# A quarter of the second expert table moved from TensorE to gathered rows and running sums on VectorE

## The chip, the core and the metric

The kernel runs on one core of one Trainium2 chip. A core has TensorE (PE in the profile, with PEld for its weight loads), VectorE (DVE), ScalarE (ACT), GpSimd (POOL) and SyncE (SP), each with its own instruction stream, and 16 DMA engines that all queues share. The engines meet only at semaphores. The metric is the device time of one execution in microseconds, as the median of several runs.

## The reference

One block of a streaming encoder on 256 tokens of width 2048 in float32. A token-mixing part (pooling and differential attention) is followed by the part that matters here, a retrieval of single-neuron experts. There are 16384 experts (128 x 128); each token picks 16 of them in each of 8 heads, so 128 per token:

```python
s1 = jnp.einsum('bshc,kc->bshk', q[..., 0, :], keys1)
s2 = jnp.einsum('bshc,kc->bshk', q[..., 1, :], keys2)
v1, i1 = lax.top_k(s1, PEER_TOPK)
v2, i2 = lax.top_k(s2, PEER_TOPK)
cand = v1[..., :, None] + v2[..., None, :]
vals, pos = lax.top_k(cand, PEER_TOPK)          # ids = i1 * 128 + i2 of the winners
gates = jax.nn.softmax(vals, axis=-1)
ug = jnp.take(u_tab, ib, axis=0)
vg = jnp.take(v_tab, ib, axis=0)
h = jnp.einsum('td,tkd->tk', xb, ug)
a = jax.nn.gelu(h, approximate=False) * gb
f = jnp.einsum('tk,tkd->td', a, vg)
```

The block then adds f and a gated embedding to the residual and normalizes each token's row of 2048 values.

## The kernel before

Nothing is gathered. The kernel computes the hidden value of every expert for every token, multiplies it by a gate that is zero for experts not picked, and multiplies the result by the whole second table.

**Units.** All weights stream through the core in units of 128 x 1024 float32 (512 KB): SP loads a unit into one of four slots of RAW, ACT rounds it to HI (L436), DVE subtracts to get the remainder LO (L713), and PE multiplies HI by the high and the low part of the activations and LO by the high part (t_unit, L1181, L1182, L1186, with the weights stationary in PE; n_unit, L1199 and L1206, with the activations stationary and the table moving). SP may load slot u % 4 when LO of unit u - 4 is made. ACT works three units ahead of PE and DVE one; LO has two slots.

**First half of U.** 64 blocks of 128 experts (two units each). ACT writes the GELU of each block to BUF (L650), which has 128 blocks of 128 experts x 256 tokens. DVE meanwhile finds the 16 winners of each head (tk0 to tk7).

**Gate stage: second half of U.** For each block of U, PE also multiplies pairs of one-hot matrices (L1435), which gives for four tokens the gates of all 128 x 128 experts. DVE makes the one-hots (L1072, L1074), multiplies GELU into BUF (L1085, from PSUM) and multiplies the gates into BUF for four tokens (L1089). After it BUF holds GELU times gate for everything. Blocks of BUF that no GELU has written yet are first filled with ones by POOL (L410, L412).

**Table stage.** 128 blocks, two units each. For block k, ACT copies BUF block k to XH (L684), DVE makes XL (L1125), each with two slots, and PE multiplies by 128 rows of the second table (in_peer_v). In the order of ACT and of DVE the split of a block stands ahead of that block's conversions, which belong to later units (vt_body). The sums stay in PSUM for the whole stage. POOL brings back the residual and the last layer norm's weights in 16 pieces (L421, L423), and at the end DVE adds the residual (L1145) and normalizes.

The order of all work is written out by hand, per engine; loops (Fori) repeat it.

## Time and profile before

| | |
|---|---|
| median of 3 runs | 2465.26 us (2464.59 to 2473.16) |
| the profiled execution | span 2465.7 us |
| PE busy | 2328.1 us (94%) |
| DVE busy | 1546.4 us (63%) |
| ACT busy | 1028.8 us (42%) |
| POOL busy | 72.6 us (3%) |
| mean DMA traffic | 172 GB/s |
| first half of U | about 868 to 1255 us |
| gate stage | about 1255 to 1688 us |
| table stage | 1692 to 2444 us |

Busy shares are means over stages with different limits; a stage is read in its own window. The end of a matmul in the profile is modelled, so the pace of PE is read from the starts of matmuls in a row. The clock that TensorE was granted is given as a share of full speed.

### The profile page before, as it was taken

How to read it: one execution, taken by the hardware profiler on the slowest of the kernel's cores; microseconds unless marked ns; L12 is line 12 of the kernel's file. 1: busy time of each engine (PE TensorE's matmuls, PEld its weight loads, DVE VectorE, ACT ScalarE, POOL GpSimd, SP SyncE). 2: the span in 40 equal slices, each digit the busy share in tenths (PEclk: the TensorE clock that was granted, in tenths of full speed). 3: DMA queues.
4: the chain of work that ended last, by engine and by line, in shares of the span. 5: the costliest groups of instructions: out<-in, count | busy, mean ns of one | idle time of the engine just before them, and what ended most of it. 6: DMA issues, size and time to landing. Idle time of an engine off the chain costs nothing.

```text
span 2465.7 us, 46080 instructions
## 1 busy us (share of the span) xinstructions
PE 2328.1 (94%) x15504; PEld 2129.6 (86%) x15504; DVE 1546.4 (63%) x2726; ACT 1028.8 (42%) x1390; POOL 72.6 (3%) x64
## 2 busy tenths in 40 slices
PE   4999999999899979999999999999999999999996
PEld 4999999898698879999999999998777777777775
DVE  4446555665744587777789889886444444444446
ACT  2444555544444434444433333333444444434442
POOL 0000000000100040000000000000000000000000
PEclk9999999999999989999999999999999999999998
DMA  6654555455455645555544554555556666665553
GB/s 176 191 183 157 183 173 173 155 179 186 152 174 162 187 158 181 181 183 182 183 140 156 159 160 154 159 160 161 180 180 184 185 188 187 189 179 187 184 187 119
DMA packets 116574, 425.25 MB, mean 172 GB/s; under 512 B 13840, under 2 KB 13856, under 8 KB 115520
## 3 DMA queue, kind: packets, MB, share of 16 engines
q1 hardware_dynamic: 112608, 412.14, 52.6%
q0 software_dynamic: 3936, 12.71, 2.1%
q8 instruction: 19, 0.31, 0.0%
q14 instruction: 11, 0.09, 0.0%
HBM read 418.50 MB, written 6.29 MB: 172 GB/s over the span
## 4 chain that ended last, share of the span: by engine, by line
PE 74%; DMA 12%; DVE 8%; issue 4%; ACT 2%; DVEq 0%; ACTq 0%; SPq 0%
PE ps L1186 17%; PE ps L1181 17%; PE ps L1182 16%; PE ps L1199 14%; DMA raw<-in_peer_v 10%; PE ps L1206 7%; DVE w_lo L713 3%; PE ps L1435 2%; DMA raw<-in_w_in 1%; DVE x_t_lo L1125 1%; ACT x_t_hi L684 1%; DMA ln_gb<-in_ln_in 1%; DVE bn L726 0%; PE ps L1307 0%; DVE tk_ab L1015 0%
## 5 line engine op out<-in xcount | busy, mean ns | idle before, releaser
L713 DVE TENSOR_TENSOR w_lo<-raw,w_hi 128x1024 fp32r<-128x1024 f32 x774 | 958.7, 1240 | 642.6 <-PE ps L1206 352.1
L436 ACT ACTIVATE w_hi<-raw 128x1024 fp32r<-128x1024 f32 x774 | 820.5, 1061 | 1118.0 <-DMA raw<-in_peer_v 371.0
L1181 PE MATMUL ps<-x_t_hi,w_hi 128*128 128x256 f32 x3328 | 836.5, 289 | 18.7 <-ACT v_t L486 12.2
L1182 PE MATMUL ps<-x_t_lo,w_hi 128*128 128x256 f32 x3328 | 821.3, 284 | 0.0
L1181 PEld LDWEIGHTS ps<-x_t_hi,w_hi 128*128 128x128 f32 x3328 | 642.2, 193 | 23.6 <-ACT w_hi L436 14.4
L1182 PEld LDWEIGHTS ps<-x_t_lo,w_hi 128*128 128x128 f32 x3328 | 642.9, 193 | 0.0
L1186 PE MATMUL ps<-x_t_hi,w_lo 128*128 128x256 f32 x3328 | 470.9, 284 | 15.3 <-DVE w_lo L713 15.3
L1186 PEld LDWEIGHTS ps<-x_t_hi,w_lo 128*128 128x128 f32 x3328 | 432.1, 193 | 16.8 <-DVE w_lo L713 16.7
L1199 PE MATMUL ps<-w_hi,x_t_hi 128*128 128x512 f32 x1024 | 324.6, 398 | 35.0 <-DVE x_t_lo L1125 34.3
L1199 PE MATMUL ps<-w_hi,x_t_lo 128*128 128x512 f32 x1024 | 317.6, 391 | 0.0
L1206 PE MATMUL ps<-w_lo,x_t_hi 128*128 128x512 f32 x1024 | 275.1, 391 | 0.0
L1199 PEld LDWEIGHTS ps<-w_hi,x_t_hi 128*128 128x128 f32 x1024 | 186.6, 188 | 100.0 <-issue 55.1
L1199 PEld LDWEIGHTS ps<-w_hi,x_t_lo 128*128 128x128 f32 x1024 | 192.9, 188 | 41.3
L1206 PEld LDWEIGHTS ps<-w_lo,x_t_hi 128*128 128x128 f32 x1024 | 193.3, 189 | 40.8
L1125 DVE TENSOR_TENSOR x_t_lo<-experts,x_t_hi 128x256 fp32r<-128x256 f32 x128 | 54.5, 426 | 114.5 <-ACT x_t_hi L684 114.5
L1089 DVE TENSOR_TENSOR experts<-ps,experts 128x512 f32 (+1 forms) x64 | 87.6, 1369 | 13.2 <-DVE experts L1085 13.1
L1199 PE MATMUL ps<-w_hi,a_hi 128*128 128x512 f32 x272 | 87.5, 403 | 8.3 <-DVE a_lo L925 4.0
L1074 DVE TENSOR_SCALAR onehots<-iota,i_t,gate_t 128x128 f32<-128x128 bf16 x256 | 92.7, 362 | 0.0
L1072 DVE TENSOR_SCALAR onehots<-iota,i_t 128x128 f32<-128x128 bf16 x256 | 77.5, 303 | 17.7 <-DVE experts L1089 13.2
L1199 PE MATMUL ps<-w_hi,a_lo 128*128 128x512 f32 x272 | 87.0, 401 | 0.0
L1435 PE MATMUL ps<-onehots 128*128 128x128 f32 x512 | 79.0, 277 | 5.0 <-DVE onehots L1074 5.0
L1206 PE MATMUL ps<-w_lo,a_hi 128*128 128x512 f32 x272 | 75.6, 400 | 0.0
(204 smaller groups left out, 1327.3 us busy)
## 6 DMA issues: line engine op xcount, KB each, us to landing
raw<-in_u SPq DMA_DIRECT2D x256, 512.0 KB, 4.6
raw<-in_peer_v SPq DMA_DIRECT2D x256, 512.0 KB, 4.9
raw<-in_w_in SPq DMA_DIRECT2D x128, 512.0 KB, 4.6
raw<-in_branch SPq DMA_DIRECT2D x32, 512.0 KB, 4.3
raw<-in_wout SPq DMA_DIRECT2D x32, 512.0 KB, 3.9
raw<-in_wq SPq DMA_DIRECT2D x32, 512.0 KB, 3.8
raw<-in_pleg SPq DMA_DIRECT2D x32, 512.0 KB, 3.7
x<-in_x SPq DMA_DIRECT2D x2, 1024.0 KB, 6.4
```

The lines of the kernel that those rows point to most:

```text
L436: nc.scalar.activation(HI[:, u % 4, :], RAW[:, u % 4, :], ACT.Copy).then_inc(hi_ready, 1)
L713: v.tensor_tensor(LO[:, u % 2, :], RAW[:, u % 4, :], HI[:, u % 4, :].bitcast(F32), ALU.subtract) \
L1072: ch.tag(v.tensor_scalar(OH[:, j % 2, r, 0, :], IOTA[:, :], I1T[:, bass.ds(t, 1)], None, ALU.is_equal))
L1074: ins = v.tensor_scalar(OH[:, j % 2, r, 1, :], IOTA[:, :], I2T[:, bass.ds(t, 1)], GATET[:, bass.ds(t, 1)], ALU.is_equal, ALU.mult)
L1089: v.tensor_tensor(dst, PS[:, 4 + c, :].rearrange("p (t e) -> p t e", t=4), dst, ALU.mult) \
L1125: v.tensor_tensor(XL[:, c, :], BUF[:, bass.ds(k, 1), :].rearrange("p a t -> p (a t)"), XH[:, c, :].bitcast(F32), ALU.subtract).then_inc(al ...
L1181: mm(o, w(HI, u % 4)[:, k, :], xh[:, ks * half + k, :], start=(s and k == 0), stop=False)
L1182: mm(o, w(HI, u % 4)[:, k, :], xl[:, ks * half + k, :], start=False, stop=False)
L1186: r = mm(o, w(LO, u % 2)[:, k, :], xh[:, ks * half + k, :], start=False, stop=(e and k == 7))
L1199: mm(nbank(tt, 2 * half + q), stn[:, tt * P:(tt + 1) * P], HI[:, u % 4, q * 512:(q + 1) * 512], start=(first and s == 0), stop=False, skip ...
L1206: r = mm(nbank(tt, 2 * half + q), ah[:, tt * P:(tt + 1) * P], LO[:, u % 2, q * 512:(q + 1) * 512], start=False, stop=last, skip_group_chec ...
L1435: r = mm(PS[:, 4 + c, o:o + P], OH[:, j % 2, t, 0, :], OH[:, j % 2, t, 1, :], start=True, stop=True)
```

## The change

The last 512 of the 2048 output columns no longer go through PE. For each token and each of its 128 picks, POOL gathers the 512 values of that expert's row of the second table (an indirect DMA for 128 tokens at a time, 256 in all), and DVE adds them, times GELU times gate, into a sum in SBUF. The GELU values that this needs are fetched by a second set of 256 indirect DMAs, 128 single values each, from a copy in DRAM of all hidden values (hidden_dram), which POOL writes block by block during U. Ids and gates are also stored in DRAM and read back once the splits of x, whose place they take, are no longer used.

Units of the table stage are 768 columns wide, and matmuls 384. XH and XL have four slots there, and each split is made two blocks ahead. In the gate stage ACT writes GELU to a tile in SBUF (GS), from which DVE multiplies and POOL writes to DRAM; PE may reuse the PSUM bank once GELU is done, where it waited for DVE's multiplication before. The one-hots are made for two tokens at a time, by three instructions in place of four. The residual and the norm's weights come back in four DMAs.

```diff
+PICKS = HEADS * TOPK
+GC = 512
+DC = D - GC
+UV = DC // 2
+NB = UV // 2
+ROWS = 8
+PICKS_FROM = 8
...
@@ gpsimd @@
             nc.gpsimd.memset(BUF[:, TOPK_CHUNKS:FIRST_ONES, :], 1.0).then_inc(ones_ready, 1)
+            for k in range(TOPK_CHUNKS):
+                pool.wait_ge(act_evac, 80 + k + 1)
+                pool.dma_start(hidden[k], BUF[:, k, :]).then_inc(h_out, 16)
+            pool.wait_ge(ids_made, 1)
+            pool.dma_start(ids_dram, IDM[:, :, :, :].rearrange("p x t r -> p (x t r)")).then_inc(stash_out, 16)
+            pool.dma_start(gate_dram, PICKED[:, 2, :, :].rearrange("p t r -> p (t r)")).then_inc(stash_out, 16)
+            pool.wait_ge(stash_out, 32)
             pool.wait_ge(picks_sb, 1)
             nc.gpsimd.memset(BUF[:, FIRST_ONES:NK, :], 1.0).then_inc(ones_ready, 1)
...
+            for c in range(NK - TOPK_CHUNKS):
+                pool.wait_ge(gelu_ready, c + 1)
+                pool.dma_start(hidden[TOPK_CHUNKS + c], GS[:, :]).then_inc(h_out, 16)
+
+            pool.wait_ge(unit_done, BASE["vtab"])
...
+            pool.wait_ge(h_out, 16 * NK)
...
+            for n in range(NT * PICKS):
+                tt, p, g = n // PICKS, n % PICKS, n // TOPK
+                if p % TOPK == 0:
+                    if g >= 2:
+                        pool.wait_ge(row_used, TOPK * (g - 2) + 1)
+                    for r in range(p, p + TOPK):
+                        pool.indirect_dma_start(out=HP[:, tt, r:r + 1], out_offset=None, in_=hidden_cells,
+                                                in_offset=bass.IndirectOffsetOnAxis(ap=IDS[:, 1, tt, r:r + 1], axis=0)
+                                                ).then_inc(h_in[g % 2], 16)
+                if n >= ROWS:
+                    pool.wait_ge(row_used, n - ROWS + 1)
+                pool.indirect_dma_start(out=ROW[n % ROWS][:, :], out_offset=None, in_=table_rows,
+                                        in_offset=bass.IndirectOffsetOnAxis(ap=IDS[:, 0, tt, p:p + 1], axis=0)
+                                        ).then_inc(row_in[n % ROWS], 16)
...
@@ scalar, gate stage @@
-                        ps = PS[:, 2 * (j // 2), 0:S]
-                        nc.scalar.activation(ps, ps, ACT.Gelu).then_inc(gelu_ready, 1)
...
+                        if c or i is not None:
+                            act.wait_ge(dve_evac, val(i, 2, 16 + c))
+                            act.wait_ge(h_out, val(i, 32, 16 * (TOPK_CHUNKS + c)))
+                        nc.scalar.activation(GS[:, :], PS[:, 2 * c, 0:S], ACT.Gelu).then_inc(gelu_ready, 1)
...
@@ scalar, table stage @@
+            def vt_body(i, c0, last):
+                for c in range(4):
+                    k = c0 + c
+                    if not (last and k + 2 >= NK):
+                        a_hi(i, k + 2)
                     for j in range(2):
...
@@ vector, gate stage @@
-                for r in range(2):
-                    t = val(i, 8, 2 * j + r)
-                    ch.tag(v.tensor_scalar(OH[:, j % 2, r, 0, :], IOTA[:, :], I1T[:, bass.ds(t, 1)], None,
-                                           ALU.is_equal))
-                    ins = v.tensor_scalar(OH[:, j % 2, r, 1, :], IOTA[:, :], I2T[:, bass.ds(t, 1)],
-                                          GATET[:, bass.ds(t, 1)], ALU.is_equal, ALU.mult)
...
+                ch.tag(v.tensor_tensor(OH[:, j % 2, :, 0, :], keys, pick_t(I1T), ALU.is_equal))
+                ch.link(v.tensor_tensor(OH[:, j % 2, :, 1, :], keys, pick_t(I2T), ALU.is_equal))
+                v.tensor_tensor(OH[:, j % 2, :, 1, :], OH[:, j % 2, :, 1, :], pick_t(GATET), ALU.mult) \
+                    .then_inc(oh_ready, 1)
...
-                v.tensor_tensor(dst, PS[:, 2 * c, 0:S], dst, ALU.mult).then_inc(dve_evac, 1)
+                v.tensor_tensor(dst, GS[:, :], dst, ALU.mult).then_inc(dve_evac, 1)
...
@@ vector, table stage @@
+            def pick(n):
+
+                tt, p = n // PICKS, n % PICKS
+                if n % TOPK == 0:
...
+                    weigh(n // TOPK)
+                dve.wait_ge(row_in[n % ROWS], 16 * (n // ROWS + 1))
+                if p == 0:
+                    ins = v.tensor_scalar(ACC[:, tt, :], ROW[n % ROWS][:, :], HP[:, tt, p:p + 1], None, ALU.mult)
+                else:
+                    dve.wait_ge(row_used, n)
+                    ins = v.scalar_tensor_tensor(out=ACC[:, tt, :], in0=ROW[n % ROWS][:, :], scalar=HP[:, tt, p:p + 1],
+                                                 in1=ACC[:, tt, :], op0=ALU.mult, op1=ALU.add)
+                ins.then_inc(row_used, 1)
...
+            for k in range(NK):
+                conv(None, 8, vb + 2 * k + DVE_LEAD)
+                upto = max(0, (k - PICKS_FROM + 1) * NT * PICKS // (NK - PICKS_FROM))
+                half = (made + upto + 1) // 2
+                for n in range(made, half):
+                    pick(n)
+                if k + 2 < NK:
+                    a_lo(None, k + 2)
+                if k + 1 < NK:
+                    conv(None, 8, vb + 2 * k + 1 + DVE_LEAD)
+                for n in range(half, upto):
+                    pick(n)
+                made = upto
...
+            ch.tag(v.tensor_tensor(RES2[:, :, DC:D], RES2[:, :, DC:D], ACC[:, :, :], ALU.add))
```

DVE in the table stage, before (the splits are L1125, the conversions L713; the other rows set registers):

```order
L1125 TENSOR_TENSOR x_t_lo<-experts,x_t_hi 128x256
L709 ISA
L712 REGISTER_ALU
L713 TENSOR_TENSOR w_lo<-raw,w_hi 128x1024
L709 REGISTER_ALU
L712 REGISTER_ALU
L713 TENSOR_TENSOR w_lo<-raw,w_hi 128x1024
```

DVE in the table stage, after, from the first pick on (the split is L1207, the conversion L785, the picks L1226 and L1229, with one row buffer per pick):

```order
L1215 TENSOR_TENSOR hidden_picked<-hidden_picked,gates 128x16
L1226 TENSOR_SCALAR gathered_sum<-row_127,hidden_picked 128x512
L1207 TENSOR_TENSOR x_t_lo<-experts,x_t_hi 128x256
L785 TENSOR_TENSOR w_lo<-raw,w_hi 128x768
L1229 SCALAR_TENSOR_TENSOR gathered_sum<-row_128,hidden_picked,gathered_sum 128x512
L785 TENSOR_TENSOR w_lo<-raw,w_hi 128x768
L1229 SCALAR_TENSOR_TENSOR gathered_sum<-row_129,hidden_picked,gathered_sum 128x512
L1207 TENSOR_TENSOR x_t_lo<-experts,x_t_hi 128x256
L785 TENSOR_TENSOR w_lo<-raw,w_hi 128x768
```

A pick now stands between each two conversions, and the loop is written out in full.

POOL from the first fill with ones on, before (L410 and L412 fill, the rest are the loads for the end):

```order
L410 MEMSET experts 128x10240
L412 MEMSET experts 128x6144
L421 DMA residual<-residual_dram 128x512 x8
L423 DMA ln_gb<-in_ln 128x512 x8
```

And after, up to the second row of the table (L446 and L455 write hidden blocks, L470 gathers single values, L475 rows):

```order
L443 MEMSET experts 128x10240
L446 DMA hidden_dram<-experts 128x256 x64
L448 DMA ids_dram<-ids_made 128x512
L449 DMA gate_dram<-picks_by_tile 128x256
L452 MEMSET experts 128x6144
L455 DMA hidden_dram<-gelu_stage 128x256 x64
L458 DMA ids<-ids_dram 128x512
L459 DMA gates<-gate_dram 128x256
L470 DMA hidden_picked<-hidden_dram,ids 128x1 x16
L475 DMA row_127<-in_peer_v,ids 128x512
L475 DMA row_128<-in_peer_v,ids 128x512
```

The second fill now stands behind the stores of ids and gates; 16 gathers of single values stand ahead of each 16 rows.

## Rows read from the trace of the kernel before

**Rows 1.** The page: span; chain that ended last, by engine and by line.

```profile
span 2465.7 us, 46080 instructions
...
PE 74%; DMA 12%; DVE 8%; issue 4%; ACT 2%; DVEq 0%; ACTq 0%; SPq 0%
PE ps L1186 17%; PE ps L1181 17%; PE ps L1182 16%; PE ps L1199 14%; DMA raw<-in_peer_v 10%; PE ps L1206 7%; DVE w_lo L713 3%; PE ps L1435 2%; DMA raw<-in_w_in 1%; DVE x_t_lo L1125 1%; ACT x_t_hi L684 1%; DMA ln_gb<-in_ln_in 1%; DVE bn L726 0%; PE ps L1307 0%; DVE tk_ab L1015 0%
```

**Rows 2.** Busy times by window (engine, count), clock, DMA share, GB/s.

```profile
1320.00:1380.00 60.00, 60.00 (x508) 60.00 (x507) 54.23 (x110) 22.36 (x27) 0.00 (x0) 1.00 0.49 157
1690.00:2440.00 750.00, 716.52 (x3057) 570.12 (x3058) 362.92 (x384) 308.71 (x382) 8.60 (x16) 1.00 0.58 182
```

**Rows 3.** The chain in order of time, inside the table stage: start, length, what.

```profile
1901.42 1.24 DVE w_lo L713
1902.84 5.07 DMA raw<-in_peer_v
...
1908.96 0.41 ACT x_t_hi L684
...
1909.52 0.44 DVE x_t_lo L1125
...
1910.08 2.10 PE ps L1199 x8
```

**Rows 4.** Timeline of TensorE: four 512-column matmuls in a row, eight 256-column ones.

```profile
1920.18 1.07 PE L1206 MATMUL ps<-w_lo,x_t_hi 128*128 128x512 f32 x4
...
1500.95 1.12 PE L1186 MATMUL ps<-x_t_hi,w_lo 128*128 128x256 f32 x8
```

**Rows 5.** Timeline: last GELU, first and last matmul of the table stage.

```profile
1688.14 0.37 ACT L672 ACTIVATE ps<-ps 128x256 f32<-128x256 f32 x1
...
1691.86 0.71 PE L1199 MATMUL ps<-w_hi,x_t_hi 128*128 128x512 f32 x2 [3.42 <-DVE x_t_lo L1125]
...
2442.57 1.07 PE L1206 MATMUL ps<-w_lo,x_t_hi 128*128 128x512 f32 x4
```

**Rows 6.** Groups by line in the table stage: count, busy us, mean ns.

```profile
L713 DVE TENSOR_TENSOR w_lo<-raw,w_hi 128x1024 fp32r<-128x1024 f32 x255 | 312.1, 1224 | 272.1 <-PE ps L1206 271.4
L1125 DVE TENSOR_TENSOR x_t_lo<-experts,x_t_hi 128x256 fp32r<-128x256 f32 x128 | 54.5, 426 | 114.5 <-ACT x_t_hi L684 114.5
```

**Rows 7.** Timeline of DVE at the end: 2048 and 1024 elements, two inputs.

```profile
2457.64 2.35 DVE L732 SCALAR_TENSOR_TENSOR residual<-residual,mean_var,ln_gb 128x2048 f32<-128x2048 f32 x1
2460.03 2.48 DVE L738 SCALAR_TENSOR_TENSOR residual<-residual,rstd,ln_gb 128x1024 f32<-128x1024 f32 x2
```

**Rows 8.** Two lines of POOL: duration of one DMA issue, minimum, median, maximum.

```profile
L421 POOL DMA_DIRECT2D residual<-residual_dram x8: 536/538/546, 1898.5 to 2102.8; - x8
...
L369 POOL DMA_DIRECT2D bias_by_rel_dram<-bias_by_rel x1: 1102/1102/1102, 21.1 to 21.1; - x1
```

**Rows 9.** Timeline of POOL and DVE side by side, at two places.

```profile
880.84 4.58 POOL L406 TENSOR_TENSOR ple_gate<-ple_gate,p_w 128x2048 f32<-128x2048 f32 x1
882.23 4.27 DVE L713 TENSOR_TENSOR w_lo<-raw,w_hi 128x1024 fp32r<-128x1024 f32 x1
...
1898.08 1.22 DVE L713 TENSOR_TENSOR w_lo<-raw,w_hi 128x1024 fp32r<-128x1024 f32 x1
1898.46 0.55 POOL L421 DMA_DIRECT2D residual<-residual_dram  x1 [629.91 <-DVE x_t_lo L1125]
```

**Rows 10.** Busy times by window: densest transfer, and TensorE after an idle stretch.

```profile
12.00:16.00 4.00, 0.00 (x0) 0.00 (x0) 1.49 (x8) 0.20 (x1) 0.00 (x0) 1.00 1.00 416
1692.00:1696.00 4.00, 4.00 (x11) 3.14 (x12) 0.74 (x1) 0.00 (x0) 0.00 (x0) 0.57 0.45 113
1696.00:1700.00 4.00, 4.00 (x19) 3.27 (x19) 2.37 (x3) 2.15 (x3) 0.00 (x0) 1.00 0.28 74
```

**Rows 11.** Timeline of DVE: the same instruction one gate-stage round apart.

```profile
1505.11 0.29 DVE L1072 TENSOR_SCALAR onehots<-iota,i_t 128x128 f32<-128x128 bf16 x1 [0.44 <-DVE experts L1089]
...
1511.44 0.29 DVE L1072 TENSOR_SCALAR onehots<-iota,i_t 128x128 f32<-128x128 bf16 x1
```

189 lines of the change are left out of this document (123 added, 66 removed).

## The prediction

> **What bounds the kernel now.** I read the page first, then windows, then the chain inside the stage that the change rebuilds. The page gives a span of 2465.7 us and a chain with PE at 74% and DMA at 12%, of which the rows of the second table (raw<-in_peer_v) are 10% of the whole span [rows 1]. The median of the runs is 2465.26 us, 0.4 us under that span, so I work on the span and correct nothing.
>
> Two stages matter. In the gate stage (the last 64 blocks of table U) PE is busy 60.00 of 60 us; it does 508 matmul records in that window, and a block takes 56 (48 of 256 columns and 8 of the one-hot products), so a block costs 6.61 us [rows 2]. In the table stage (V), PE is busy 716.52 of 750 us, DVE 362.92, and the DMA engines 0.58 of their time at 182 GB/s [rows 2]. It lasts from the first matmul at 1691.86 to 2442.57 + 1.07 = 2443.64, thus 751.8 us for 256 units [rows 5], 2.94 us each. Back to back, four 512-column matmuls end 1.07 us after the first starts and one lasts 0.39, so one starts every 0.227 us; twelve are 2.73 us and 256 units 699 us [rows 4]. The missing 53 us are a wait that the chain shows: lo of a slot done, a load of 5.07 us, then ACT comes late to the activation split (x_t_hi at 1908.96), DVE after it (x_t_lo at 1909.52), and only then PE at 1910.08 [rows 3]. ACT works in order, so the split for block c stands behind a conversion that waits for a load.
>
> **The change, part by part.**
>
> *Narrower products.* A unit has 768 columns in place of 1024, so its twelve matmuls have 384. Eight 256-column matmuls end after 1.12 us, one lasts 0.28, so they start every 0.120 us [rows 4]; 384 lies halfway between 256 and 512, which gives 0.1735 us, 2.08 a unit, 533 us for the stage. That is the floor by PE, 219 us under today's 751.8.
>
> *Four activation slots.* Each split is now made two blocks ahead, so the wait of [rows 3] has a block's time to spare; I count it as gone, it is inside the 219. What is late next is below: DVE and what feeds it.
>
> *DVE in the table stage.* A conversion of 1024 takes 1.224 us [rows 6]; 2048 elements take 2.35 and two of 1024 take 2.48, thus about 1.24 each, so an element costs about 1.08 ns [rows 7] and 768 take 0.95. A pick (scalar_tensor_tensor, 512 elements) is 1.24 less 512 times 1.08 ns, thus 0.69. A block (two units) has two conversions 1.90, a split 0.43 and, from block 8 on, 256/120 = 2.13 picks 1.47: 3.8 us against PE's 4.16. DVE fits with 9% to spare and is not the bound, if nothing it waits for is late. But the picks stand in its order between the conversions, as the order of DVE shows: a pick that waits for its row holds back the next conversion, and PE waits for that one about two units later.
>
> *POOL.* It now issues 512 gathers, 256 of one hidden value per token and 256 of a 2 KB row per token, in groups: 16 of the first, then 16 of the second. The trace holds no gather. Below it is bounded by an ordinary issue of 128 rows, 0.538 us; above by the largest issue there, 1.102 us [rows 8], plus one whole DVE instruction of 1.22 waited for each time, 2.32. A gather has to fetch 128 separate addresses before it can write descriptors, so I place it by the heavier row, a little under it: T = 1.0 us. With only 8 row buffers the groups don't run free. Of a group, POOL's 16 + 1 issues pass before its first row is asked for, about 2.6 us before that row and DVE's own step are there, then DVE must use 7 rows (one each 1.95 us, which is 4.16/2.13) before the last of the 16 rows can be issued: a group takes 18T + 2.6 + 0.7 + 13.7, or 32T where that is more. For T = 1.0 that is 35.0 us; PE alone would take 16 times 1.95 = 31.2. POOL begins with the last GELU (1688.1 [rows 5]) and the first pick is due at block 8, 33.3 us into the stage, by when the first group's values are there. The stage: 33.3 + 15 times 35.0 + 31.2 = 590 us.
>
> *The clock.* Each of the 15 groups ends in a stall of some 4 us. After today's wait of 3.42 us at the start of this stage [rows 5] the granted clock was 0.57, thus at the lower of the two levels for most of the window, and 11 matmuls ran in 4 us in place of 19 [rows 10]: 8/19 of 4 us, 1.7 us lost. Fifteen times is 25 us: 615 us. Low end nothing, if PE's own lead shortens the stall; high end the same again.
>
> *Gate stage.* DVE's round lasts 1511.44 - 1505.11 = 6.33 us [rows 11], PE's 6.61 [rows 2], so DVE has 0.28 to spare. Four one-hot instructions of 128 become three of 256, of which the third waits for the second. At 0.43 us for 256 elements [rows 6], with the next starting 0.09 before an end as now, I get 0.34 + 0.47 + 0.34 = 1.15 against 0.91 now, 0.24 more, twice a block: DVE's round becomes 6.81, PE waits 0.2, 64 blocks 13 us. Ends: nothing, if two-byte inputs go faster, and 30 us. The hidden blocks that POOL writes to DRAM lie beside this; GELU waits for that write, but it has most of 6.6 us. Where the stage begins, POOL now writes ids and gates out and waits for them before it fills the ones, about 3 us later than now (a landing and two issues, an estimate from the 5.07 us of a larger transfer [rows 3]), and DVE's first spread waits for it: 3 us. In the first half of U, 64 writes of 128 KB lie beside a saturated PE and cost nothing while POOL is idle, as it is; without that cover they would cost 0.54 each.
>
> *End.* One more addition of 1024 elements (1.24), the eight closing additions a quarter narrower: 0 to +1; I take 0.
>
> *Sum.* 2465.7 - 751.8 + 615 + 13 + 3 = 2345 us.
>
> **A rule that speaks against it.** The rows come first: a conversion under way beside a POOL tensor operation took 4.27 us, the normal one beside an ordinary DMA issue of POOL 1.22 [rows 9]. So POOL and DVE can shut each other out, and a plain issue does not. The Trainium skill (SBUF — State Buffer, section SBUF: two separate sides) says that a DVE instruction with two SBUF inputs shuts out a GpSimd operation only if that one reads SBUF, and that whoever starts first holds the ports to its end. By that rule the trace agrees for both rows, and the open question is whether a gather, which takes its ids from SBUF, counts as reading. That is the second rival.
>
> **The rivals.**
>
> *A: gathers are as cheap as plain issues.* For it: 0.538 us is the only price of a 128-row issue [rows 8]. Against: those rows have fixed addresses. Up to T = 0.79 a group fits in 31.2 us, and PE sets the pace: 2465.7 - 751.8 + 537 + 13 + 3 = 2267.
>
> *B: the DMA engines become the bound.* The stage must move 100.7 MB of table and 67.1 MB of gathered rows. At today's ratio (182 GB/s for a share of 0.58, thus 314 at 1.0 [rows 2]) that is 534 us; at the densest window, 416 GB/s [rows 10], 403. On top come 32768 single values, 2048 for each engine, whose price no row shows; a 4 KB packet costs 0.58 x 16 x 750 / 32640 = 0.21 us [rows 2], so 0 to 430 us. At 0.05 each, 100 us: a stage of 635, a kernel of 2365. For it: loads already take 5.07 us from issue to landing [rows 3]. 
>
> *C: slower. Gathers and DVE's two-input instructions take turns.* Each gather must wait for the DVE instruction under way to read its ids, or holds DVE up. Place: POOL, in every block from 8 on. POOL alone needs 512T, so the stage reaches today's 751.8 less the 16 of the other terms at T = 1.44; above that the change loses. With half a DVE instruction (0.6) on top of 1.0, T = 1.6 and the stage is 819 us: 2465.7 - 751.8 + 819 + 16 = 2549. If they exclude each other wholly, a block is 3.8 + 4.27 x 1.0 = 8.1 us, 120 of them and the first 33 make 1002 us: 2732. At the far bound, T = 2.32, POOL alone makes 1188 us and the kernel 2918. For it: [rows 9], and a DVE that is busy 90% of the time. Against: the plain issue beside a conversion, which neither felt.
>
> *D: no change.* T falls between 1.42 and 1.46: within 12 us of 2465.
>
> **How the numbers follow.** My forecast (POOL sets the pace with T from 0.8 to 1.4, 2280 to 2450) has 0.42, A 0.14, B 0.12, C 0.28, D 0.04. Faster are forecast, A and B: 0.68; same is D, 0.04; slower C, 0.28. About 0.5%, 12 us, is what a measurement of this kernel can tell from no change. The time is 2345. The range goes from 2258, a little under A, to 2550, the mild form of C; what lies beyond (the hard forms of C, about 0.14, and something under A, about 0.04) is under 0.2. The likeliest case alone is 2280 to 2450.
>
> **What would show it.** Right: POOL busy near 100% through the table stage with gathers of about 1.0 us each; DVE's longest waits at the picks, for rows landing, once in 16; PE waiting for DVE's conversions, with dips of the clock; table matmuls starting every 0.17 us; conversions of about 0.95 us; no wait of PE for x_t_lo. A would show as POOL waiting for DVE and PE busy all through; B as a DMA share at 0.95 or more, with ACT waiting for loads; C as gathers of 1.5 us and more, or conversions well over 1 us in the table stage while POOL is idle or waiting. In the gate stage PE should show short waits for one-hots; if it is busy 60 of 60, my 13 us are wrong. The forecast as a whole is wrong if a gather is under 0.8 or over 1.44 us.

## The result and the profile after

The changed kernel takes 2482.45 us, the median of 5 runs (2480.02 to 2486.09). The kernel before took 2466.75 beside it. The ratio is 1.0053, 95% interval 1.0037 to 1.0068: slower by half a per cent, where 2345 was forecast. The profiled execution has a span of 2481.1 us.

The page first: span, and the chain that ended last, to be held against [rows 1].

```profile
span 2481.1 us, 46379 instructions
...
PE 46%; POOL 20%; DVE 13%; issue 11%; DMA 7%; ACT 1%; DVEq 1%; SPq 0%; ACTq 0%
PE ps L1302 12%; PE ps L1297 12%; PE ps L1298 12%; POOL hidden_picked L470 10%; POOL row L475 9%; PE ps L1317 6%; DVE w_lo L785 4%; PE ps L1324 3%; DVE experts L1171 3%; DMA raw<-in_u 2%; DMA raw<-in_peer_v 1%; DVE onehots L1158 1%; DMA raw<-in_w_in 1%; DMA row<-in_peer_v,ids 1%; DVE onehots L1157 1%
```

POOL had no share of the chain; now it has 20%, and about half of "issue" (11%) stands with it. Inside the stage (1718 to 2460) the chain is POOL for 65%, issue for 20% and PE for 4.5%. The windows answer [rows 2]: busy time and count of PE, PE's weight loads, DVE, ACT and POOL, then granted clock, DMA share, GB/s.

```profile
1320.00:1380.00 60.00, 58.81 (x481) 57.21 (x480) 53.09 (x86) 20.99 (x25) 4.85 (x9) 1.00 0.52 173
...
1718.00:2460.00 742.00, 570.44 (x3066) 564.68 (x3064) 457.32 (x658) 251.60 (x378) 557.10 (x516) 0.88 0.71 230
```

In the table stage no engine looks full by its busy time, not even POOL with 557 of 742. The groups of that stage say why (count, busy us, mean ns of one, then idle time ahead of them and what ended it):

```profile
L475 POOL DMA_INDIRECT row<-in_peer_v,ids x256 | 283.8, 1109 | 92.2 <-issue 74.0 <-DVE gathered_sum L1229 16.8 <-DVE gathered_sum L1226 1.3
...
L470 POOL DMA_INDIRECT hidden_picked<-hidden_dram,ids x256 | 271.1, 1059 | 81.8 <-issue 77.7 <-DMA gates<-gate_dram 4.1
L785 DVE TENSOR_TENSOR w_lo<-raw,w_hi 128x768 fp32r<-128x768 f32 x255 | 244.5, 959 | 49.8 <-PE ps L1324 39.3 <-ACT w_hi L496 7.9
L1324 PE MATMUL ps<-w_lo,x_t_hi 128*128 128x384 f32 x1024 | 236.9, 355 | 168.2 <-DVE w_lo L785 168.2
...
L1229 DVE SCALAR_TENSOR_TENSOR gathered_sum<-row,hidden_picked,gathered_sum 128x512 f32<-128x512 f32 x254 | 189.7, 747 | 45.0 <-DMA row<-in_peer_v,ids 43.1
```

A gather is 1.08 us long on average, and 0.30 us pass between two with nothing to wait for (the 77.7 and 74.0 us of "issue"). All told (283.8 + 92.2 + 271.1 + 81.8) the 512 gathers take 729 us, 1.42 each: 1.08 of length, 0.30 of pause and 0.04 of waits for DVE and for the gates. POOL is thus occupied nearly all the time, but the pauses don't count as busy. The stage, by PE's first and last matmul in the timeline:

```profile
1716.17 0.59 PE L1317 MATMUL ps<-w_hi,x_t_hi 128*128 128x384 f32 x2 [3.28 <-DVE x_t_lo L1207]
...
2455.78 0.86 PE L1324 MATMUL ps<-w_lo,x_t_hi 128*128 128x384 f32 x4
```

That is 740.5 us in place of 751.8 [rows 5]. The row of gathers runs from 1719.06 to 2446.04, 727 us of them; 2.9 us lie ahead of it and 10.6 behind. A group of 32 takes 43.9 to 45.1 us, except the first (51.4, where rows wait for the first pick at block 8) and the eighth (53.1, where POOL also sends the four loads for the end). The chain in order of time, in one group of 32 gathers (start, length, what), shows a gather every 1.25 us or more and hardly anything else (some of the 0.30 us pieces of "issue" are left out):

```profile
1999.83 0.30 issue
2000.13 1.23 POOL hidden_picked L470
2001.66 1.21 POOL hidden_picked L470
2002.87 0.30 issue
2003.18 0.95 POOL hidden_picked L470
...
2010.91 0.94 POOL hidden_picked L470
2012.16 0.94 POOL hidden_picked L470
2013.41 0.95 POOL row L475
```

DVE stands still meanwhile, from 2004.79 to 2014.68, waiting for the group's hidden values (15 such waits, 154 us), and PE waits for DVE's conversion (16 times, 168 us). The lengths vary from 0.94 to 1.71. The short ones fall where DVE is idle: 135 of the 512 have no DVE instruction beside them, and their mean is 0.944, their longest 0.95, for single values and for rows of 2 KB alike.

In the gate stage a block now takes some 7 us, by DVE's round. Its timeline, against [rows 11]:

```profile
1505.55 0.42 DVE L1157 TENSOR_TENSOR onehots<-iota,i_t 128x256 f32<-128x256 bf16 x1 [0.43 <-DVE experts L1171]
1505.89 0.42 DVE L1158 TENSOR_TENSOR onehots<-iota,i_t 128x256 f32<-128x256 bf16 x1
1506.44 0.42 DVE L1159 TENSOR_TENSOR onehots<-onehots,gate_t 128x256 f32<-128x256 f32 x1
1506.78 1.22 DVE L785 TENSOR_TENSOR w_lo<-raw,w_hi 128x1024 fp32r<-128x1024 f32 x1
...
1512.42 0.43 DVE L1157 TENSOR_TENSOR onehots<-iota,i_t 128x256 f32<-128x256 bf16 x1
```

From one round's start to the next are 6.87 us here, and some 7.2 in each second round, against 6.61 for PE in a block before; three one-hot instructions take 1.23 us (1505.55 to 1506.78), against 0.91 for the four before. The table stage starts 24.3 us later than before (1716.17 against 1691.86).

So the 15 us are: 24 more up to the stage, 11 less in it, 2 more behind it.

### The profile page after: what moved, and what is told of

Same layout as the page of the kernel before. It is cut to its first block, busy times and chain, and to the rows that moved or that the text cites. A ratio compares the mean times of both kernels' runs of the same rounds, so it can differ in the third digit from the quotient of the medians.

```text
span 2481.1 us, 46379 instructions
## 1 busy us (share of the span) xinstructions
PE 2197.0 (89%) x15504; PEld 2128.1 (86%) x15504; DVE 1655.5 (67%) x2876; ACT 974.5 (39%) x1390; POOL 692.5 (28%) x697
## 4 chain that ended last, share of the span: by engine, by line
PE 46%; POOL 20%; DVE 13%; issue 11%; DMA 7%; ACT 1%; DVEq 1%; SPq 0%; ACTq 0%
PE ps L1302 12%; PE ps L1297 12%; PE ps L1298 12%; POOL hidden_picked L470 10%; POOL row L475 9%; PE ps L1317 6%; DVE w_lo L785 4%; PE ps L1324 3%; DVE experts L1171 3%; DMA raw<-in_u 2%; DMA raw<-in_peer_v 1%; DVE onehots L1158 1%; DMA raw<-in_w_in 1%; DMA row<-in_peer_v,ids 1%; DVE onehots L1157 1%
## 5 line engine op out<-in xcount | busy, mean ns | idle before, releaser
L496 ACT ACTIVATE w_hi<-raw 128x1024 fp32r<-128x1024 f32 (+1 forms) x774 | 766.0, 990 | 1173.4 <-DMA raw<-in_peer_v 467.6
L785 DVE TENSOR_TENSOR w_lo<-raw,w_hi 128x1024 fp32r<-128x1024 f32 (+1 forms) x774 | 891.0, 1153 | 423.2 <-PE ps L1302 258.1
L1324 PE MATMUL ps<-w_lo,x_t_hi 128*128 128x384 f32 x1024 | 236.9, 355 | 168.2 <-DVE w_lo L785 168.2
L475 POOL DMA_INDIRECT row<-in_peer_v,ids x256 | 283.8, 1109 | 92.2 <-issue 74.0
L470 POOL DMA_INDIRECT hidden_picked<-hidden_dram,ids x256 | 271.1, 1059 | 81.8 <-issue 77.7
L1317 PE MATMUL ps<-w_hi,x_t_hi 128*128 128x384 f32 x1024 | 271.8, 347 | 3.3 <-DVE x_t_lo L1207 3.3
L1317 PE MATMUL ps<-w_hi,x_t_lo 128*128 128x384 f32 x1024 | 270.0, 345 | 0.0
L1229 DVE SCALAR_TENSOR_TENSOR gathered_sum<-row,hidden_picked,gathered_sum 128x512 f32<-128x512 f32 x254 | 189.7, 747 | 45.0 <-DMA row<-in_peer_v,ids 43.1
L455 POOL DMA_DIRECT2D hidden_dram<-gelu_stage x64 | 34.5, 540 | 408.0 <-ACT gelu_stage L735 400.0
L446 POOL DMA_DIRECT2D hidden_dram<-experts x64 | 34.5, 540 | 317.4 <-ACT experts L710 317.4
```

Source lines behind the costliest of these rows:

```text
L446: pool.dma_start(hidden[k], BUF[:, k, :]).then_inc(h_out, 16)
L470: pool.indirect_dma_start(out=HP[:, tt, r:r + 1], out_offset=None, in_=hidden_cells, in_offset=bass.IndirectOffsetOnAxis(ap=IDS[:, 1, tt, ...
L475: pool.indirect_dma_start(out=ROW[n % ROWS][:, :], out_offset=None, in_=table_rows, in_offset=bass.IndirectOffsetOnAxis(ap=IDS[:, 0, tt, p ...
L496: nc.scalar.activation(HI[:, u % 4, 0:width], RAW[:, u % 4, 0:width], ACT.Copy).then_inc(hi_ready, 1)
L785: v.tensor_tensor(LO[:, u % 2, 0:width], RAW[:, u % 4, 0:width], HI[:, u % 4, 0:width].bitcast(F32), ALU.subtract).then_inc(lo_ready, 1)
L1229: ins = v.scalar_tensor_tensor(out=ACC[:, tt, :], in0=ROW[n % ROWS][:, :], scalar=HP[:, tt, p:p + 1], in1=ACC[:, tt, :], op0=ALU.mult, op1 ...
```

## The experiments

Each ratio is to the kernel before on the same chip. The runs were made on five chips, and times from different chips are compared by these ratios.

### Only the four slots

```diff
 # on the kernel before
-        nc.scalar.activation(XH[:, c, :], BUF[k]...)      # split for block c, when block c is next; 2 slots
+        nc.scalar.activation(XH[:, c % 4, :], BUF[k + 2]...)   # split two blocks ahead; 4 slots
```

> The kernel before, with one part of the change alone: four activation slots in the table stage and each split made two blocks ahead; units stay 1024 wide, nothing is gathered. My theory: the stage of before lost 53 us to the late split, so this part alone brings the table stage from 752 to about 700 us and the kernel to 2412. Rival: the wait behind the split was the load's latency and comes back at the next conversion: under 10 us gained, 2455 or more.

Measured: 2415.52 us, ratio 0.9819 (0.9803 to 0.9836). The window in the stage, columns as above:

```profile
1740.00:2240.00 500.00, 500.00 (x2207) 414.05 (x2206) 258.83 (x277) 223.27 (x276) 7.52 (x14) 1.00 0.66 200
```

PE waits for nothing any more. The term "the wait is gone" was right: the stage is 698.2 us long in the trace, 700 were expected, and the kernel is 44 us faster than the one before (2459.2 on this chip) without any gather.

### No gathers at all, in two steps

```diff
 # (a) on the changed kernel: each gather by an ordinary DMA of its size
-  pool.indirect_dma_start(out=HP[:, tt, r:r+1], in_=hidden_cells, in_offset=IDS[:, 1, tt, r:r+1])
+  pool.dma_start(HP[:, tt, r:r+1], hidden[r, :, tt:tt+1])
-  pool.indirect_dma_start(out=ROW[n % 8], in_=table_rows, in_offset=IDS[:, 0, tt, p:p+1])
+  pool.dma_start(ROW[n % 8], a["peer_v"][:, p, DC:D])
 # (b) the rows as in (a), and the 16 hidden values of a group by one DMA
+  pool.dma_start(HP[:, tt, p:p+16], hidden[p, :, 0:16])
```

> The changed kernel with each of its 512 gathers replaced by an ordinary DMA of POOL that moves the same number of pieces of the same sizes (128 single values, 128 rows of 2 KB) from fixed places; the output is not the reference's. My theory: the change lost to POOL's time for a gather (1.08 us and 0.30 us between two). With 0.54 us each POOL needs 32 x 0.54 = 17 us a group, PE sets the pace, the table stage falls from 741 to about 545 and the kernel to some 2285. Rival: the transfers themselves (DMA engines, small pieces) or DVE's picks set the pace; then the stage stays above 690 and the kernel above 2430.

> The changed kernel without any gather: each of the 256 rows is fetched by an ordinary DMA of the same size from fixed places (one 2 KB piece in each of 128 table rows that lie 1 MB apart), and the 16 hidden values of a group by one ordinary DMA (which leaves out the 32768 single cells). Beside the earlier run with all 512 replaced by ordinary DMAs, at 2382, this leaves out the single cells only. If it was the 4-byte cells, sent 16 DMAs in 8.6 us, that crowded the DMA engines there and made the table loads late, the kernel now takes about 2288 with PE busy all through the stage. If it was the regular 1 MB step of the rows, it stays at about 2380 with ACT waiting for raw by 300 us and more and PE for w_hi.

Measured: (a) 2382.14 us, ratio 0.9691 (0.9671 to 0.9711); (b) 2330.03 us, 0.9481 (0.9465 to 0.9497). Both missed their forecasts on the slow side, (a) by 97 us, (b) by 42. Still, (a) has as many instructions, pieces and bytes as the changed kernel and differs from it in the kind of issue (and in the places read), and it is 100 us faster. So the time that the changed kernel lost lies in POOL's price for a gather. The windows of (a) and (b):

```profile
1740.00:2240.00 500.00, 453.96 (x2455) 429.68 (x2453) 364.97 (x530) 202.64 (x306) 223.56 (x422) 0.98 0.90 279
```

```profile
1740.00:2240.00 500.00, 479.60 (x2651) 462.61 (x2651) 393.31 (x573) 219.44 (x330) 131.65 (x245) 0.99 0.93 301
```

In (b) the DMA engines are 93% occupied, and PE waits for ACT's copies of late loads. Single cells cost 52 us (a less b); the rest of the miss goes with the ordinary rows, since the next run gathers the rows, moves as many bytes of them and is faster. How the fixed 1 MB step of their places does that, no run told. With cheap issues it is the DMA engines that come next, as the second rival had it: at a share of 1.0 they would move 301/0.93, 324 GB/s.

### Half of the gathers

```diff
 # on the changed kernel: only the 256 gathers of rows are left
-  16 x pool.indirect_dma_start(out=HP[:, tt, r:r+1], ...)
+  pool.dma_start(HP[:, tt, p:p+16], hidden[p, :, 0:16])
```

> The changed kernel without its 256 gathers of single values: each group's 16 come by one ordinary DMA from a fixed place, so the output is not the reference's. The 256 gathers of rows stay. My theory: half of POOL's 1.38 us times 512 goes; 256 gathers need 353 us, under PE's 533, and the stage falls to about 550, the kernel to 2290. Rival (rows are what costs: 2 KB pieces on busy DMA engines, or DVE and POOL taking turns at the gathers of rows): the stage stays over 640, the kernel over 2380.

> The changed kernel without the 256 gathers of hidden cells (16 values by one ordinary DMA for each group of 16, which leaves the single cells out), again: 2294 us before, with all signals at once. Rows are gathered one by one, each after a wait for DVE. Theory 1 (late signals need many gathers without a pause on POOL): 2294 within 10 also where the yardstick of this call has late signals. Theory 2 (any gather beside units of 768 columns): over 2340 there.

Measured: 2294.53 us, ratio 0.9326 (0.931 to 0.9341), and on another chip 2292.37 us, 0.9306 (0.9291 to 0.9322). The window of the first:

```profile
1740.00:2240.00 500.00, 493.62 (x2795) 482.58 (x2794) 416.29 (x605) 230.55 (x348) 299.71 (x258) 1.00 0.92 315
```

PE is busy 99%. PE's pitch, DVE's load and the transfers of the rows hold at the pace that the forecast asked for. This run leaves out the 32768 single cells together with their 256 gathers; the run before tells the two apart: with the cells but cheap issues it is 2382, with the gathers 2482. What keeps the changed kernel back is first of all POOL's 512 gathers.

### Only hidden gathers

```diff
 # on the changed kernel: the 256 hidden gathers stay
-  pool.indirect_dma_start(out=ROW[n % 8], in_=table_rows, ...)
+  pool.dma_start(ROW[n % 8], a["peer_v"][:, p, DC:D])
```

> The changed kernel with the 256 gathers of hidden cells, 16 in a row, and each of the 256 rows by an ordinary DMA of the same size from fixed places (so other rows are summed). POOL's time is 256 x 1.38 + 256 x 0.54 = 491 us of gathers and issues, under PE's 533, so it should be near the run with no gather at all (2330), to 2345. Where the yardstick has late signals, theory 1 (gathers without a pause) says that they appear here in each row of 16, and the time goes over 2370; if they don't, it takes more than 16 in a row.

Measured: 2580.84 us, ratio 1.0483 (1.0466 to 1.0501): far off, though POOL has less to do (all signals of TensorE come at once here, see the section on late signals). Its timeline over one group, first POOL, then DVE:

```profile
1989.57 1.23 POOL L470 DMA_INDIRECT hidden_picked<-hidden_dram,ids  x1 [0.30 <-issue]
...
2005.31 4.36 POOL L475 DMA_DIRECT2D row<-in_peer_v  x8
...
2026.43 0.54 POOL L475 DMA_DIRECT2D row<-in_peer_v  x1 [7.68 <-DVE gathered_sum L1227]
```

```profile
2006.73 0.18 DVE L1213 TENSOR_TENSOR hidden_picked<-hidden_picked,gates 128x16 f32<-128x16 f32 x1 [9.77 <-DMA hidden_picked<-hidden_dram,ids]
2009.78 0.75 DVE L1227 SCALAR_TENSOR_TENSOR gathered_sum<-row,hidden_picked,gathered_sum 128x512 f32<-128x512 f32 x1 [2.87 <-DMA row<-in_peer_v]
...
2024.51 0.96 DVE L783 TENSOR_TENSOR w_lo<-raw,w_hi 128x768 fp32r<-128x768 f32 x1 [6.60 <-ACT w_hi L494]
```

While 16 hidden gathers stand in a row, DVE runs out of rows and waits 9.77 us. Then 8 rows of 256 KB go out in 4.36 us, DVE waits 2.87 us for the first, and a conversion soon waits another 6.60 for a load. That load took 11.97 us from issue to landing (it landed at 2023.54), and the DMA engines were full meanwhile (share 0.98 and more from 2010 to 2025), so it stood behind the rows by all that shows. The next hidden gathers must wait until DVE has worked the rows off. The group takes 51 us. By the forecast's group formula (16 gathers, two issues, a landing, DVE's pace for seven rows) it would be some 41; DVE's waits for ACT, behind late loads, are 154 us in the stage, some 10 a group, about what is missing. So batches and late loads together can undo the change with POOL far from full; by this estimate the batches alone, at 41 us a group and 16 groups, would not. The expectation, which added up POOL's time only, overlooked what the prediction had in it.

### Other one-hots

```diff
 # on the changed kernel, per block half: the kernel before's four instructions
-  onehot1 (256), onehot2 (256), onehot2 *= gate (256)
+  for r in 0, 1:  onehot1 (128);  onehot2 and gate in one tensor_scalar (128)
```

> The changed kernel with the one-hots of before (four instructions of 128 with I2T in float32, in place of three of 256); some small tiles share space with the one-hots so that it fits. My theory: DVE's round in the gate stage (6.87 to 7.1 us) is over PE's 6.61 because of the one-hots, so the stage gives back about 25 us: the kernel at 2457. Rival: the new waits of GELU (for DVE's multiplication and for the write to DRAM) hold the round; then it stays within 5 us of 2482.

> The changed kernel with the one-hots of the kernel before, again, as the yardstick of this call: it has all 512 gathers and took 2463 us where TensorE's signals came at once. Theory P (late signals belong to the chip, with all of these gathers): it is either 2463 within 10, with every signal within 0.1 us, or 2540 to 2600 with signals up to 16 us late. If it falls between, the state is no matter of two kinds.

Measured: 2463.35 us, ratio 1.0014 (1.0004 to 1.0025), and 2463.58 us, 1.0003 (0.9993 to 1.0012). The window in the gate stage:

```profile
1320.00:1380.00 60.00, 60.00 (x505) 59.74 (x505) 54.04 (x109) 22.02 (x27) 4.85 (x9) 1.00 0.54 176
```

PE is full again, with POOL still writing the hidden blocks out, and the table stage starts at 1692.05, 24.1 us earlier. Against the changed kernel that is 10 us by the first ratios (1.0053 and 1.0014) and 17 by those of the later runs (1.0074 and 1.0003). The 25 us that were expected come back in the stage's start, but not wholly in the kernel's time, and no run tells why. The loss in this stage is the one-hots', not the writes'.

### What DVE does to a gather

```diff
 # (a) on the changed kernel: the running sum over one column in place of 512
-  v.scalar_tensor_tensor(out=ACC[:, tt, :],   in0=ROW[n % 8],         ...)
+  v.scalar_tensor_tensor(out=ACC[:, tt, 0:1], in0=ROW[n % 8][:, 0:1], ...)
 # (b) on the version of the last experiment, with the second token tile's gathers too: 512 again,
 #     units of 1024 columns, second tile's rows summed over one column only
```

> The changed kernel with each of DVE's running sums over 512 columns cut to one column (all but one of the gathered columns are left out of the sum); all 512 gathers, conversions, splits and waits stay. Theory 1 (a gather lasts 0.94 us alone and longer beside DVE's two-input instructions, with 0.30 us between two whatever DVE does): DVE's busy time in the table stage falls from 457 to about 290 us, the mean gather from 1.08 to about 1.02 us, pitch 1.32, the stage to some 690 us and the kernel to about 2431. Rival (a gather's length has nothing to do with DVE; 1.2 and more come from the DMA side): the gathers keep a mean of 1.08 us and the kernel stays within 8 us of 2482. Third (only the running sums, with three inputs, lengthen a gather): the mean falls to 0.94 us, the kernel to about 2390.

> The changed kernel with the running sums of DVE cut to one column, again, beside the unaltered one on one chip. By theory 1 (late signals belong to the chip or placement) it moves with the unaltered kernel: where that is near 2482 and has no late signals, this one has none either and takes about 2431, as first forecast (mean gather 1.02 us); where that is over 2540, this one is near 2596. By theory 2 it is 2596 whatever the unaltered one does.

> The version that gathers the last 512 columns for the first 128 tokens only, units 1024 wide, but with all 512 gathers as in the changed kernel; the second half of the rows is fetched and not summed over (one column of each only). POOL is the bound again: 512 x 1.38 to 1.42 = 707 to 727 us, plus 14 as in the changed kernel, so the kernel takes 2465.7 - 751.8 + 5 + 721 to 741 = 2440 to 2460 where signals come at once. Where the yardstick has late signals: if it is the number of gathers without a pause that makes them late, they are late here too, and the kernel takes over 2500; if it is the 768-column units, they are not, and it stays under 2465.

> Units 1024 wide, all 512 gathers, the second half of the rows not summed, again; 2518 us where signals came at once. If the yardstick has late signals here, the number of gathers without a pause as the cause puts this one over 2560; the narrow units as the cause leave it at 2518 within 10. If the yardstick has none: 2518 within 10, and the question stays open.

Measured: (a) 2595.94 us, ratio 1.0553 (1.0536 to 1.0571), again 2597.91 us, 1.0573 (1.0555 to 1.059); (b) 2518.14 us, 1.0228 (1.0211 to 1.0245), again 2515.2 us, 1.0181 (1.016 to 1.0202). The time of (a) is not DVE's doing: beside the unaltered kernel on the same chip (2589.82) it is 8 us more, and it is taken up in the section on late signals. What the sums cost in time where signals come at once, no run shows; the length of a gather can be read all the same. First the gathers of single values of (a) (its rows are as long, 1042), then both kinds of (b):

```profile
L470 POOL DMA_INDIRECT hidden_picked<-hidden_dram,ids x256 | 266.7, 1042 | 81.3 <-issue 77.7 <-DMA gates<-gate_dram 3.6
```

```profile
L475 POOL DMA_INDIRECT row<-in_peer_v,ids x256 | 309.2, 1208 | 96.1 <-issue 71.6 <-DVE gathered_sum L1232 18.7 <-DVE gathered_sum L1228 5.8
L470 POOL DMA_INDIRECT hidden_picked<-hidden_dram,ids x256 | 297.4, 1162 | 81.3 <-issue 77.7 <-DMA gates<-gate_dram 3.6
```

With less on DVE a gather is 1.04 us long, with longer conversions (1.22 in place of 0.96) 1.18, against 1.08; alone it is 0.94. (b) missed its expectation of 2440 to 2460, by 58 us and more, mostly for that reason: 512 times 0.10 more are 51 us. The 0.30 us between two stay in all. How it comes about stands in the traces instruction by instruction. POOL and DVE in the version of the last experiment (units 1024 wide, 256 gathers, second run):

```profile
1845.15 1.31 POOL L470 DMA_INDIRECT hidden_picked<-hidden_dram,ids  x1 [0.30 <-issue]
1846.76 1.73 POOL L470 DMA_INDIRECT hidden_picked<-hidden_dram,ids  x1 [0.30 <-issue]
1848.80 0.94 POOL L470 DMA_INDIRECT hidden_picked<-hidden_dram,ids  x1 [0.31 <-issue]
1850.05 1.60 POOL L470 DMA_INDIRECT hidden_picked<-hidden_dram,ids  x1 [0.30 <-issue]
```

```profile
1844.42 1.23 DVE L785 TENSOR_TENSOR w_lo<-raw,w_hi 128x1024 fp32r<-128x1024 f32 x1 [0.45 <-PE ps L1329]
1846.45 1.22 DVE L785 TENSOR_TENSOR w_lo<-raw,w_hi 128x1024 fp32r<-128x1024 f32 x1 [0.81 <-PE ps L1329]
...
1849.62 1.22 DVE L785 TENSOR_TENSOR w_lo<-raw,w_hi 128x1024 fp32r<-128x1024 f32 x1
```

The three long gathers end at 1846.46, 1848.49 and 1851.65; the conversions under way when they began end at 1845.65, 1847.67 and 1850.84. The distance is 0.81, 0.82 and 0.81 us. So a gather that starts while a DVE instruction is under way ends 0.82 us after that instruction (or takes 0.94 where that is more), and any other takes 0.94. With "under way" as "begun at least 0.04 us before the gather", this rule gives the length of each of the 512 gathers of the changed kernel to 0.007 us on average (correlation 0.97), and of the 256 in that version's first run to 0.003. In the changed kernel it holds for all three kinds of DVE instruction there: 296 gathers found one under way and last 1.19 on average; 81 had one that began with them or later and last 0.947; 135 had none and last 0.944.

Hardly anything comes the other way. In the changed kernel 188 conversions began inside a gather and last 0.954 us, as do the 28 that began in a pause; only 34 that began within 0.04 us of a gather's start last 0.99. So the third rival's mechanism is there, at 0.14 us for a gather on average, not 0.6.

### The gathers interleaved

```diff
 # on the changed kernel
-  per group: 16 hidden gathers, then 16 rows
+  16 hidden gathers once; then in turn one row, one hidden gather for the group after
```

> The changed kernel with the gathers in another order: after a first group of 16 hidden cells, each row gather is followed by one hidden gather for the group after, instead of 16 hidden gathers in a row ahead of each group. Number and kind of the 512 gathers stay. Theory 1 (POOL's total sets the pace: 512 gathers, each 1.08 us long on average with 0.30 us between two, thus 1.38): POOL keeps nothing to wait for, the stage is about 5 + 512 x 1.38 + some us for the last picks = 715 us, against 741 in the changed kernel, and the kernel takes about 2457; the once-in-16 waits of DVE of up to 12 us become many short ones, the sum of DVE's waits for gathers falls from 197 us by no more than 30. Theory 2 (the grouping as such costs, as in the group formula of the prediction where a group waits for its own rows): with the grouping gone PE would set the pace, and the kernel would fall under 2350. If the steadier use of DVE makes each gather longer, 1.15 us and more, the time stays at 2480.

> The changed kernel with its gathers interleaved (one of a hidden cell, one of a row), again, beside the unaltered one on one chip. By theory 1 it takes about 2457 where the unaltered one is near 2482, and about 2560 where that is over 2540. By theory 2 it is 2562 whatever the unaltered one does.

Measured: 2562.3 us, ratio 1.0416 (1.0396 to 1.0436), again 2557.31 us, 1.0403 (1.0373 to 1.0433). Beside the unaltered changed kernel on the same chip (2589.82, next section) that is 32 us less, near the 25 that were forecast as a difference; the time itself was missed by 105, for the reason that follows. The kernel did not fall under 2350 with the grouping gone, so the grouping is not what costs most. Both runs had late signals; the interleaving without them was not measured.

### Late signals

Cut sums and interleaving both came out some 100 us over expectation. Their traces showed something that no earlier trace had, so the unaltered changed kernel was run beside them on another chip, and once more on a third.

> The changed kernel once more, not altered, on the same chip as the two below. In the runs with interleaved gathers and with cut running sums, TensorE's signal that a unit is done came up to 16 us after the unit's last matmul while gathers stood in a row, and both kernels came out at 2562 and 2596 against 2459 for the kernel before; in the changed kernel's own trace the signal always came within 0.02 us. The first late signals stand ahead of the first running sum, where the programs do the same work. Theory 1 (the lateness comes with gathers in a row on that chip or placement, not with the edits): if this call shows it at all, it shows it here too, and the changed kernel takes over 2540. Theory 2 (it comes with the edits): 2482 again, within 10.

> The changed kernel, not altered, a third time, as the yardstick of this call. By the calls so far it has one of two states: 2482 within 12, every signal of TensorE within 0.1 us of its matmul, or 2590 within 15 with signals up to 20 us late. A third value would end the talk of two states.

Measured: 2589.82 us, ratio 1.0535 (1.0518 to 1.0553), and 2486.87 us, 1.0074 (1.0046 to 1.0101). The same program costs 5% on one chip and under 1% on others; the kernel before took 2457 and 2469 on these two chips. The timeline of the slower execution, PE, DVE, ACT:

```profile
1805.31 1.65 PE L1324 MATMUL ps<-w_lo,x_t_hi 128*128 128x384 f32 x4 [3.16 <-issue]
...
1808.44 0.51 PE L1317 MATMUL ps<-w_hi,x_t_lo 128*128 128x384 f32 x2
1818.76 1.65 PE L1324 MATMUL ps<-w_lo,x_t_hi 128*128 128x384 f32 x4 [9.80 <-issue]
```

```profile
1817.74 0.96 DVE L785 TENSOR_TENSOR w_lo<-raw,w_hi 128x768 fp32r<-128x768 f32 x1 [11.82 <-remote]
```

```profile
1817.67 0.84 ACT L496 ACTIVATE w_hi<-raw 128x768 fp32r<-128x768 f32 x1 [12.30 <-remote]
```

PE finished a unit at 1806.96. DVE and ACT, which need that unit's buffers, start only at 1817.7, together, and name no releaser; PE then waits for DVE. The record of PE's signal "unit done" stands at 1817.65, 10.7 us behind the matmul that carries it. All that time POOL issued gathers, one every 1.25 us. In that execution 130 of the 256 signals are more than 0.1 us late, up to 20.9 (in 20 of them DVE went on before the record, so there only the record is late); the first is 8 us into the stage, before any running sum. In the traces at 2482 and 2487 us all 256 come within 0.1 us.

On two of the five chips signals were late, in all five runs there that had 512 gathers: both of the cut sums, both of the interleaving, and this one. The version of the next section (256 gathers, units 1024 wide) and the one with ordinary rows ran on one of these chips and were not held up; of the former's 256 signals 47 have no record of their own, but DVE always went on 0.11 us after the matmul. The kernels that share a chip were run together and the programs are the same elsewhere, so it goes with the chip or with something else that such a set of runs has in common. Whether it needs 768-column units or only many gathers was to be told by the second run with 1024-column units, but that chip showed no late signals. It stays open.

### Gathered columns for the first 128 tokens only

```diff
 # on the changed kernel with the one-hots of before; nothing is left out of the result
+  units 1024 wide again; the last 512 columns of tokens 128..255 by matmuls: 21 of 24 in a block
-  for n in range(NT * PICKS):    # 512 gathers
+  for n in range(PICKS):         # 256 gathers
```

> A version that computes everything but moves less to POOL and DVE: the last 512 columns come by gathered rows for the first 128 tokens only; TensorE keeps them for the other 128 tokens (21 of 24 matmuls of 512 columns in a block, units 1024 wide again), with four activation slots and the one-hots of the kernel before. Half the gathers: 256. Theory: POOL needs 256 x 1.38 = 353 us and is hidden, DVE 2.44 + 0.43 + 1.07 x 0.75 = 3.7 us a block, PE 21 x 0.227 = 4.77 us a block, 610 us; the stage 612 us, the kernel 2465.7 - 751.8 + 612 + 5 for the stage's start = 2331 us. Rival (what keeps PE back in the changed kernel is gathers as such beside the table loads, not their total on POOL): loads come late, PE waits for w_hi or w_lo, and the kernel is over 2370.

> The version that gathers the last 512 columns for the first 128 tokens only (256 gathers, units 1024 wide, nothing left out), again, to set it beside the changed kernel on one chip: 2336 within 10 in either state, since TensorE's signals came at once in it also on a chip where the changed order of gathers had late ones; thus a ratio of about 0.95 to the kernel before and 0.90 to 0.94 to the changed one.

Measured: 2336.54 us, ratio 0.951 (0.9489 to 0.9531), on the chip on which gathers in a row had late signals, and 2336.71 us, 0.9461 (0.9438 to 0.9485), beside the changed kernel's 2486.87 (0.940 of it, by the medians). The window of the second:

```profile
1800.00:2200.00 400.00, 396.74 (x1746) 326.90 (x1745) 292.09 (x346) 201.12 (x250) 213.85 (x178) 1.00 0.86 290
```

PE is busy 99%, and POOL waits 199 us for DVE to free row buffers, thus it has time to spare. This version beats both kernels, by 5% and 6%. Of the 5%, the four slots alone give 1.8 (first experiment), so the gathered half is worth 3 to 4.

## Why the prediction was wrong

The forecast was 2345, 136 us under the profiled 2481; the stage accounts for 126 (740.5 against 615), the way to it for 8, the end for 2.

**The step that failed** is the size of T under "POOL": "I place it by the heavier row, a little under it: T = 1.0 us". A gather takes 0.94 us alone, 0.14 more on average beside DVE, and 0.30 us pass before the next: 1.38 from start to start, and 1.42 with the few waits. The rows used as bounds, ordinary issues, have nothing between two, and the 0.30 was in no term. With T = 1.38 the prediction's own formula gives 32T = 44.2 for a group, which 13 of the 15 measured groups take within 1 us, and 33.3 + 15 x 44.2 + 31.2 = 727 us for the stage, where 740.5 were measured. With that and no clock term its sum is 2457; the last 24 us are the 13 of the two longer groups and the ends, 8 on the way to the stage and 2 behind it. The mechanism, its place and DVE's and PE's waits once in 16 were as described; the size of one term was not.

T lay inside the stated bounds of 0.54 to 2.32, and under 1.44, of which the text says "above that the change loses". That point was set by 512T alone and leaves out the ends; by the group formula of the same text the gain is gone at T = 1.40. And two signs were badly put: "POOL busy near 100%" could not come true with a pause that doesn't count as busy (557 of 742 us), and "if a gather is under 0.8 or over 1.44 us" did not fire at a length of 1.08, though the forecast was wrong, since the length is not the pitch.

**The clock term** (25 us) was counted on top. The granted clock did fall, to 0.88 in the stage, but where POOL sets the pace PE's slower matmuls lie under its wait: all of PE is 4.5% of the stage's chain, 33 us. It should have been near nothing in that case.

**The batches.** That a group waits for its own rows was right as a formula, but at T = 1.38 the other branch, 32T, decides. With hidden gathers only, the group's own rows decide, and that run, with its late loads, ends 251 us over the one with no gather (2581 against 2330).

**The slots** were right (the wait is gone, 44 us by themselves). So were the narrow matmuls (four take 0.85 us with one lasting 0.33, a pitch of 0.173), the conversion (0.96 us against 0.95) and the split; a pick takes 0.75 against 0.69.

**The gate stage** was forecast at 13 us, with 3 for its start, and lost 24 up to the next stage's start. Three one-hots take 1.23 us, not 1.15: the third starts 0.55 after the second, since it waits for it, not 0.47. And the block takes DVE's round plus a little at the loop's end.

**The rivals.** C ("the second rival" in the passage on the rule) was right in kind and not in price: gathers do wait for DVE, but on average by 0.14 us, not 0.6, and DVE does not wait for them. The Trainium skill (SBUF — State Buffer, section SBUF: two separate sides) says that a DVE instruction with two SBUF inputs and a GpSimd operation that reads SBUF exclude each other, and the first one holds the ports to its end. The traces agree for the gather that waits. They do not agree the other way: the 188 conversions that began inside a gather last 0.954 us, no longer than those that began in a pause, so a gather under way does not hold DVE off in this case. D put no change at T from 1.42 to 1.46; T was 1.42 with the waits in it, and the result, 15 us over the profiled time of before, lies on its edge. A would have needed T under 0.79. B is real only where issues are cheap: at the pace of A the DMA engines stand at 0.92 to 0.93.

**The chances.** Slower had 0.28, and the same 0.04 in a band of 24 us around a point that the working itself named. A term bounded from 0.54 to 2.32, on which everything hung, deserved a wider middle.

## What to carry to other kernels

Work that moves to POOL's gathers pays there for each instruction, not for its bytes (0.944 us alone for 4 bytes an index as for 2 KB): count the instructions, take the pitch from start to start with the gap in it, and if the queue's total comes near the stage's time, nothing is won however much the other engines save. Move only so much that the slower partner has time to spare: here half of the gathers, with POOL waiting for DVE a third of the stage, went with 5% off, and all of them with none. And a batch of a kind that its consumer can't use yet needs buffers for the whole time it lasts.

## What the hardware showed unexpectedly

- An indirect DMA of 128 indices occupies POOL for 0.94 us, and two in a row are never closer than 0.30 us; an ordinary DMA takes 0.54 with no gap (8 in 4.36 us).
- A gather that starts at least 0.04 us after a DVE instruction began and before it ends lasts until 0.82 us after that instruction's end, up to 1.71 us in all in the changed kernel. A DVE instruction that starts inside a gather is not held (a conversion lasts 0.954 us, as in a pause).
- On two of five chips TensorE's signals came late while gathers stood in a row, up to 20.9 us in the changed kernel. The changed kernel then took 2590 us in place of 2482; the kernel before showed no difference.
- Eight ordinary row transfers sent within 4.36 us were followed by a wait of 6.60 us for a table load.
